# Output stage of a hybrid encoder block: the split activations kept in pieces of 32 tokens instead of 16

## The reference, cut to what matters

```python
z = jnp.einsum('thed,td->the', expert_u[eidx], tb)
act = (gates * jax.nn.gelu(z.astype(jnp.float32))).astype(tb.dtype)
return jnp.einsum('the,thed->td', act, expert_v[eidx])
```

## Time and profile before

| | us |
|---|---|
| median of 3 runs | 4347.16 |
| lowest and highest of them | 4347.15, 4352.74 |
| the profiled execution's own time | 4347.39 |
| its span, first to last instruction | 4345.8 |
| output stage in it, first to last matmul on `x_split_o` | 3342.2 to 4326.1 |

### The profile page before, as it was taken

One profiled execution on the slowest core, in us unless ns is written; L12 is line 12 of the kernel. 1 busy time (PEld: TensorE's weight loads), 2 busy tenths in 40 slices (PEclk: granted clock), 3 DMA queues, 4 the chain that ended last, 5 costly groups with the idle time before them and its releaser, 6 DMA issues.

```text
span 4345.8 us, 65461 instructions
## 1 busy us (share of the span) xinstructions
PE 4269.3 (98%) x24970; PEld 3904.0 (90%) x24970; DVE 3410.7 (78%) x4173; ACT 1286.6 (30%) x1230; POOL 917.9 (21%) x804
## 2 busy tenths in 40 slices
PE   8999999999999999999999999999999999999998
PEld 5778887989989888887889999999999999999998
DVE  5776766788888844555897999987776989999996
ACT  4222222221222232222223444432333323333333
POOL 0111111000100020011111333344441222222223
PEclk9999999999999999999999999999999999999999
DMA  6888887799888986989844888999997989999995
GB/s 221 302 290 303 288 309 247 252 286 292 282 291 286 320 301 216 306 283 343 282 151 146 325 326 336 354 385 370 370 363 277 353 334 371 362 383 378 376 353 192
DMA packets 395168, 1326.18 MB, mean 305 GB/s; under 512 B 29472, under 2 KB 202528, under 8 KB 279360
## 3 DMA queue, kind: packets, MB, share of 16 engines
q1 hardware_dynamic: 298352, 892.67, 59.3%
q0 software_dynamic: 62224, 391.99, 22.8%
q10 hardware_dynamic: 34496, 40.37, 2.6%
HBM read 1130.49 MB, written 328.53 MB: 336 GB/s over the span
## 4 chain that ended last, share of the span: by engine, by line
PE 81%; DVE 9%; issue 3%; DMA 3%; SPq 1%; POOL 1%; ACT 0%; DVEq 0%; POOLq 0%; ACTq 0%
PE bank L833 26%; PE bank L834 26%; PE bank L835 25%; DVE w_lo L1567 2%; DMA u_rows<-u_turned_c 2%; DVE u_row L2103 1%; DVE hot_j L2113 1%; PE bank L933 1%; PE bank L940 1%; DVE u_turned_c L1574 1%; DVE hot_i L2109 1%; SPq L443 1%; PE bank L1069 1%; PE bank L909 1%; POOL cand L731 0%
## 5 line engine op out<-in xcount | busy, mean ns | idle before, releaser
L833 PE MATMUL bank<-x_hi,w_hi 128*128 128x352 f32 (+2 forms) x5760 | 1942.7, 337 | 15.3 <-DVE w_lo L1567 6.9
L834 PE MATMUL bank<-x_lo,w_hi 128*128 128x352 f32 (+2 forms) x5760 | 1931.0, 335 | 0.0
L835 PE MATMUL bank<-x_hi,w_lo 128*128 128x352 f32 (+2 forms) x5760 | 1929.0, 335 | 0.0
L1154 ACT ACTIVATE w_hi<-w_raw 128x2048 fp32r<-128x2048 f32 x432 | 827.1, 1915 | 1987.9 <-PE bank L835 1887.7
L1567 DVE TENSOR_TENSOR w_lo<-w_raw,w_hi 128x2048 fp32r<-128x2048 f32 x432 | 995.0, 2303 | 259.1 <-ACT w_hi L1154 256.9
L833 PEld LDWEIGHTS bank<-x_hi,w_hi 128*128 128x128 f32 x5760 | 1085.5, 188 | 119.5 <-issue 28.9
L834 PEld LDWEIGHTS bank<-x_lo,w_hi 128*128 128x128 f32 x5760 | 1084.8, 188 | 85.0 <-issue 2.6
L835 PEld LDWEIGHTS bank<-x_hi,w_lo 128*128 128x128 f32 x5760 | 1085.5, 188 | 82.6
L834 PE MATMUL bank<-x_split_o,w_hi 128*128 128x352 f32 x2048 | 657.1, 321 | 0.0
L833 PE MATMUL bank<-x_split_o,w_hi 128*128 128x352 f32 x2048 | 655.5, 320 | 0.8 <-DVE z_group L1992 0.8
L835 PE MATMUL bank<-x_split_o,w_lo 128*128 128x352 f32 x2048 | 654.5, 320 | 0.0
(11 more groups left out here) (309 smaller groups left out, 2849.1 us busy)
## 6 DMA issues: line engine op xcount, KB each, us to landing
v_rows<-v_blocks SPq DMA_DIRECT2D x128, 1024.0 KB, 10.3
w_raw<-u_blocks SPq DMA_DIRECT2D x128, 1024.0 KB, 6.9
w_raw<-v_blocks SPq DMA_DIRECT2D x128, 1024.0 KB, 7.3
w_raw<-w_proj SPq DMA_DIRECT2D x112, 1024.0 KB, 7.3
u_raw_a<-u_blocks SPq DMA_DIRECT2D x99, 1024.0 KB, 8.3
u_rows<-u_turned_a SPq DMA_DIRECT2D x396, 256.0 KB, 5.6
g_scratch<-g_chunk SPq DMA_DIRECT2D x11, 2048.0 KB, 13.2
z_scratch<-z_stage POOLq DMA_DIRECT2D x112, 176.0 KB, 5.3
```

The source lines that it names most:

```text
L833: pe.matmul(dst, whi, xhi, start=start, stop=False)
L834: pe.matmul(dst, whi, xlo, start=False, stop=False)
L835: return pe.matmul(dst, wlo, xhi, start=False, stop=stop)
L1154: act.activation(WH[s][:, :], RAW[s][:, :], ACT.Copy).then_inc(w_hi, 1)
```

## The change

A tile of 352 tokens is now 11 pieces of 32 tokens (128 bytes), 2240 bytes apart. The 16 tiles of a group (8 K-tiles, `hi` and `lo`) lie side by side in each 2240 bytes: tile `t` at `128*t`, with 192 bytes left over. The two groups take 24832 bytes each. The whole begins 32 bytes later (byte 4256; the weights' first byte is 128 above a multiple of 256, this one 160), and `v_row1`, `v_row2` lie 992 bytes lower. The matmuls, their number, widths and order are the same, and so are the weights and their places; on all five engines the order of instructions is what it was, with the shape `11x32` where `11x2x16` stood. One wait has another value: all eight `act_hi` of group 0 now wait until row 11 of `x_hi` (counted from 0) has been read, since every tile reaches over all of the 24640 bytes.

```diff
-PIECE = 16
-ROWS = 12
-TILES = 3
+PIECE = 32
+ROWS = NT // PIECE
+PITCH = 2 * GJ * PIECE + 48
+SPAN = (ROWS * PITCH + 63) // 64 * 64
...
-    (XSO, VG1, VG2), e13 = lay(xh_at, [("x_split_o", [P, (2 * KT + TILES - 1) // TILES, 2, ROWS, TILES, PIECE], F32R),
-                                       ("v_row1", [P, D], F32), ("v_row2", [P, D], F32)])
+    xo_at = xh_at + (raw_at - xh_at + 32) % 256
+    (XSO, VG1, VG2), e13 = lay(xo_at, [("x_split_o", [P, 2, SPAN], F32R), ("v_row1", [P, D], F32),
+                                       ("v_row2", [P, D], F32)])
...
-    def x_o(kk, lo):
-        t = 2 * kk + lo
-        return XSO[:, t // TILES, :, 0:NT // (2 * PIECE), t % TILES, :].rearrange("p i j e -> p j i e")
+    def x_o(par, jj, lo):
+        t = 2 * jj + lo
+        return XSO[:, par, 0:ROWS * PITCH].rearrange("p (j n) -> p j n", n=PITCH)[:, :, t * PIECE:t * PIECE + PIECE]
 
     def in_pieces(a):
-        return a.rearrange("p (j i e) -> p j i e", i=2, e=PIECE)
-
-    def old_tile(kk):
-        return (8 * ROWS * TILES * PIECE * ((2 * kk + 1) // TILES + 1) - 1) // (4 * L)
+        return a.rearrange("p (j e) -> p j e", e=PIECE)
+
+    x_o_old = (xo_at - xh_at + 4 * ROWS * PITCH - 1) // (4 * L)
...
             for jj in range(GJ):
-                act_hi(0, jj, jj + 1, x_free, 4 * (KT - 1) + old_tile(jj) + 1)
+                act_hi(0, jj, jj + 1, x_free, 4 * (KT - 1) + x_o_old + 1)
```

More of the change, by code:

```diff
@@ L1090, in out_block @@
                         m = mm3(o_bank[u][k][:, 0:NT], WH[u][:, wcol], WL[u][:, wcol],
-                                x_o(GJ * par + jj, 0), x_o(GJ * par + jj, 1), jj == 0, jj == GJ - 1)
+                                x_o(par, jj, 0), x_o(par, jj, 1), jj == 0, jj == GJ - 1)
                 m.then_inc(w_used, 1)
@@ L1472, in act_hi @@
                 act.wait_ge(sem_, free)
-                act.activation(x_o(GJ * par + jj, 0), in_pieces(ZG[par][:, jj, :]), ACT.Copy).then_inc(x_hi, 1)
+                act.activation(x_o(par, jj, 0), in_pieces(ZG[par][:, jj, :]), ACT.Copy).then_inc(x_hi, 1)
             for jj in range(GJ):
-                act_hi(0, jj, jj + 1, x_free, 4 * (KT - 1) + old_tile(jj) + 1)
+                act_hi(0, jj, jj + 1, x_free, 4 * (KT - 1) + x_o_old + 1)
             gelu_kept(NB_E - 1)
@@ L2137, in product_lo @@
                 dve.wait_ge(x_hi, x0 + jj + 1)
-                dve.tensor_tensor(x_o(GJ * par + jj, 1), in_pieces(ZG[par][:, jj, :]), x_o(GJ * par + jj, 0).bitcast(F32),
+                dve.tensor_tensor(x_o(par, jj, 1), in_pieces(ZG[par][:, jj, :]), x_o(par, jj, 0).bitcast(F32),
                                   ALU.subtract).then_inc(x_lo, 1)
```

## The result

| | before | after |
|---|---|---|
| median us (runs) | 4347.15 (4) | 4377.14 (4) |
| lowest and highest us | 4346.9, 4352.74 | 4372.8, 4383.1 |
| profiled execution, its span | 4347.39, 4345.8 | 4372.8, 4371.2 |
| first to last matmul on `x_split_o` | 983.9 | 1008.6 |

The ratio is 1.0067 (95% interval 1.0049 to 1.0084): the changed kernel is slower by 0.7%, and 4377.14 us lies above the whole range that was given (to 4362).

What follows compares the result with a forecast made beforehand. PE was taken as the bound. 4347.4 - 1.5 (slow K-tile) + 1.9 (wait) + 1.1 (clock) = 4348.9 us, less 0.2 to the median: 4348.7 us, +0.04%. Own range 4342 to 4355, whole range 4334 to 4362.

Steps and rivals of the forecast that it cites:

- What bounds the kernel: PE, busy 978.6 of 981 us in the output stage; 1 ns on each of 6144 matmuls is 6.1 us.
- Instructions: Number, order and widths stay; ACT's and DVE's splits gain 8 and 3 ns at most, off the bound: nothing.
- (a): Moving reads, 11 jumps for 22: at most 34.5 us less, taken as zero because straight tiles are slower.
- (b): Moving reads against the weight load beside each matmul: taken as zero, bounds +11 us and -17 us.
- straight rate: Z stage's 159.7 ns per matmul with tiles in one run; +1.8 ns, +11 us, taken as upper bound.
- (c): Odd groups' slow K-tile 2, blamed on pieces either side of byte 32768: loss goes, 1.5 us less.
- The wait at the changeover: Group 0's splits on ACT wait for row 11, so PE restarts 1.9 us late, near 3344.1.
- The clock after that pause: PE idle 2.7 us at the changeover, then one fall to half clock: 1.1 us more, bounds 0 and 2.4.
- B: Rival, output stage: longer pieces collide like a straight run, 11 us more, 4360 us; far end 4374; chance 0.26.
- D: Rival: layout is nothing to PE, only wait and clock remain, 4350.2 us; chance 0.12.

Runs made afterwards that it cites:

- e6: Changed kernel with pieces 2176 bytes apart (even groups) and 2304 (odd) instead of 2240: 160.0 / 164.5 ns per matmul, total 4378.95 us.
- e8: Old pieces of 16 tokens in the changed kernel's address order modulo 256 (even groups), second half 128 on (odd): 163.1 / 163.3 ns, 4381.92 us.
- e7: Changed kernel, split weights and all after w_raw 64 bytes on, pieces 128 (even) / 192 (odd) from weights modulo 256: 162.2 / 166.7 ns, 4392.07 us.
- e9: Changed kernel with a weight load of 32 columns instead of 128: 161.1 ns in both kinds of group, 4380.77 us.
- f1: Changed kernel, pieces 192 (even) / 0 (odd) bytes from weights modulo 256, weight load of 32 columns: 160.0 / 163.0 ns, 4372.83 us.
- f4: Kernel before, each piece of 16 beginning 64 bytes back (even groups) or 32 back (odd) modulo 256: 163.3 / 159.5 ns, 4376.8 us.
- g1: Kernel before with a stretch's tiles 256 bytes apart instead of 64, all at place 0: 155.6 ns, median 4338.99 against 4355.16 us, ratio 0.9977.
- e10: Kernel before with a weight load of 32 columns instead of 128: 158.6 / 158.4 ns (even / odd groups), 4349.06 us.
- e2: Changed kernel with pieces 96 (even groups) / 128 (odd) bytes from the weights modulo 256 instead of 32: 162.2 ns in both, 4384.69 us.
- e3: Changed kernel with pieces 160 (even groups) / 192 (odd) bytes from the weights modulo 256 instead of 32: 163.8 / 166.6 ns, 4399.34 us.
- e5: Changed kernel with pieces 2048 bytes apart (even groups) and 2112 (odd) instead of 2240: 164.5 / 165.6 ns, 4397.61 us.
- e1: Changed kernel with pieces 0 (even groups) / 64 (odd) bytes from the weights modulo 256 instead of 32: 164.4 / 162.3 ns, 4383.36 us.
- e4: Changed kernel with pieces 224 (even groups) / 32 (odd, unchanged) bytes from the weights modulo 256: 162.2 ns in both, 4377.75 us.
- e12: Kernel before, with the step after each pair of pieces 0 (even groups) or 64 forward (odd) instead of 64 back: 165.8 / 166.9 ns, 4404.39 us.
- f2: Kernel before's order, hi at 0 and lo at 64 (even groups), both at 0 (odd), halves 25344 bytes apart: 157.8 / 155.6 ns late, 4347.55 us.
- f3: Kernel before's order, hi 64 and lo 0 (even groups), hi 128 and lo 64 (odd), halves 25344 bytes apart: 158.8 / 157.9 ns, 4366.95 us.
- g2: Kernel before with all tiles at place 64 from the weights modulo 256: 155.6 ns, median 4351.59 against 4355.16 us, ratio 0.9998.

## Why the prediction was wrong, point by point

**What bounds the kernel: right.** 1 ns on each matmul was put at 6.1 us. Measured: 4.0 ns in the trace and 24.6 us in the stage.

**Instructions: right.** The splits kept their cost and order; DVE is busy 883.2 us of the stage (882.0 before), ACT 302.2 (303.6):
```profile
3345.00:4351.00 1006.00, 1003.73 (x6186) 1003.41 (x6185) 883.20 (x807) 302.17 (x266) 268.19 (x177) 1.00 0.88 337
```

**(a) Jumps cost nothing: right.** e6's even groups have eleven pieces and the rate of a straight tile, and e8 has the old 22 pieces and about the new rate.

**(b) The pattern against the weight load: this step failed.** It took zero, because a step of 64 back was kept, and bounded the loss by the straight rate, +1.8 ns or 11 us. The loss was 4.0 ns, 24.6 us. The two reads do act on each other (e7 with e9 and f1), so the kind of effect was right. What was wrong is to take the slope for a sufficient reason: e8 and f4's odd groups have it too, and stand at 163.1 and 159.5. The text saw the difference ("a piece sweeps 128 bytes once instead of 64 bytes twice") and set it aside in favour of the row nearest. And the straight tile was no upper bound: it is one order among others, and most kernels of the table are slower than it.

**(c) The slow K-tile: right in its size, wrong in its cause.** It was 11 to 13 ns slower than its neighbours (582 ticks of 1/1.2 ns against 566 to 569), as the 12 taken. But byte 32768 did not make it. In g1 the same tile lies over that byte, also with pieces on both sides of it in turn, and its K-tile takes 560 ticks like all others. And e10 moves the slow one to other K-tiles with all moving addresses kept: there it is even K-tile 2, none of whose bytes lies near that address. (In the kernel before, only the first four of the tile's eleven pairs lie on either side of the byte, not all as the prediction reads.) The 1.5 us were no gain of their own; every K-tile became as slow as that one, 0.486 us.

**The wait at the changeover: right.** Forecast 1.9 us, measured 2.1 (last Z matmul to first output matmul 1.1 us before, 3.2 after). ACT and DVE of after, as the earlier trace rows, then PE, as the earlier trace rows:
```profile
3338.27 3.21 ACT L1474 ACTIVATE x_split_o<-z_group 128x352 fp32r<-128x352 f32 x8 [3.46 <-PE bank L836]
3341.39 1.90 ACT L1155 ACTIVATE w_hi<-w_raw 128x2048 fp32r<-128x2048 f32 x1
```
```profile
3338.80 3.57 DVE L2139 TENSOR_TENSOR x_split_o<-z_group,x_split_o 128x352 fp32r<-128x352 f32 x8 [2.05 <-ACT x_split_o L1474]
3342.29 0.52 DVE L1993 TENSOR_TENSOR z_group<-bank,rstd_b 128x352 f32<-128x352 f32 x1
```
```profile
3337.85 0.32 PE L836 MATMUL bank<-x_hi,w_lo 128*128 128x352 f32 x1
...
3339.77 0.32 PE L836 MATMUL bank<-x_hi,w_lo 128*128 128x352 f32 x1
3342.96 0.43 PE L834 MATMUL bank<-x_split_o,w_hi 128*128 128x352 f32 x1 [2.87 <-DVE z_group L1993]
```
The eight splits are one piece, begun 0.42 us after the third matmul of row 11 (3337.85), as worked out; PE stands still for 2.87 us (forecast 2.7). The 0.2 us more are DVE's: its eight `product_lo` take 3.57 us in a row where ACT's eight take 3.21, so they end last by their own pace and not by ACT's eighth, which the prediction followed. The weight split and the evacuation behind it are hidden, as was said.

**The clock after that pause: 0 by luck, and the fall was priced too low.** Forecast +1.1 us, measured 0. In after, the window behind the restart holds 21 matmuls at the upper level, and only the later stretch, which the kernel before has too, is at half:
```profile
3345.00:3348.00 3.00, 3.00 (x21) 1.00 1.10 382
...
3549.70:3556.40 6.70, 6.70 (x29) 0.50 0.94 371
```
Other executions did fall at this very pause. The restart of e2, and the window around it:
```profile
3350.74 0.66 PE L836 MATMUL bank<-x_split_o,w_hi 128*128 128x352 f32 x1 [2.84 <-DVE z_group L1995]
```
```profile
3350.00:3356.70 6.70, 5.96 (x20) 0.50 0.93 335
```
e2, e3 and e9 fell to half after 2.8 us of idle time and e5 after 2.4, while after, e1, e4, e6, e7 and f1 kept the upper level after 2.8 to 2.9. The last Z block before the pause is the same in all of them, and so is the work behind it, but for the layout and the shorter load of e9 and f1. So neither the idle time nor the work around it tells whether the clock falls; what does stays open. Where it fell, the first output block took 1.2 us (e9) to 2.8 us (e2) longer than the second, 0.1 of it also without a fall. The forecast's 1.1 lies at the lower end, and e2 is beyond its bound of 2.4; its fall is most of the 4.1 us by which its stage is longer than that of after at the same interval. It was read off a window of 13 matmuls, of which ten are of the kind `bank<-hot_j,hot_i` with 128 columns: no measure for matmuls of 352.

**The rivals.** B named the right sign and, at its far end (162 ns, +25 us, 4374 us), the size: that end was read off the slow K-tile, whose rate every K-tile now has. Its reason, longer pieces that collide like a straight run, falls with e6 (straight order, 160.0) and e8 (short pieces, 163.1). The range cut B at the straight rate; with that far end inside it would have held the profiled time, and 4377 us still not. D, that the layout is nothing to PE, is refuted. The Trainium skill says in "SBUF — State Buffer", section "Who interferes with whom", that PE's two read ports are independent and that PE never waits. Here, with instructions and transfers alike, the interval reached from 155.6 (g1) to 166.9 ns (e12) with only the addresses changed, and the measurement decides. The 149.2 ns that D took from the Trainium skill, "TensorE: Matmul & The Clock Gate", section "Back-to-back issue gap", is given there for an isolated matmul and not for a stream with weight loads, so it does not say that this stage has no surplus; no kernel here came below 155.6.

## What to carry to other kernels

Where PE is the bound and streams its moving tile beside a weight load, the addresses of the moving tile modulo 256 bytes can be worth several per cent of the interval: 7% between the best and the worst here, for fp32r and 352 columns. Best was to have all moving tiles at one place. Take any new layout as unknown until its rate is measured, and measure it in several stretches and more than one execution, since one layout can have two rates. Count matmuls in a window rather than compare totals, which spread by more than most of these effects. And when a layout's rate is to be bounded, the other pattern at hand is a sample, not an upper bound; a cause inferred from the address of one slow tile wants an experiment of its own.

## What the hardware showed beyond that

**A rhythm in whole ticks.** The intervals are not a smooth average. In the changed kernel the three matmuls of a K-tile start 157.5, 165.8 and 163.3 ns apart, 584 ticks of 1/1.2 ns in all, in every group and every K-tile on average. g1 has 560 ticks, the straight order 576, the kernel before 566 to 572 with a slow one of 582. It looks as if the stream settles into a repeating state.

**One layout, two rates.** That state does not follow from the addresses alone. f2's odd groups went from 160.0 to 155.6 ns with the pause of PE in group 3 between, the code and all addresses being the same. Even groups changed as well: 162.2 in group 0 and 163.8 from group 2 on in e3, 167.8 and 165.6 in e12, 157.8 and 158.9 in f3. What was traced in two executions came out alike in both, though: 162.2 at place 32 (after, e4) and at 128 (e2, e7), 166.6 and 166.7 at 192 (e3, e7), 155.6 with all tiles at one place (g1, g2). The kernel before was traced once, but the times of all its runs, up to 4360.15 us, and those of the changed kernel, from 4372.8, do not overlap, so the loss stands. f2's change of 4.4 ns is as large as that loss, though: a kernel that was traced once (e5, e6, e8, e12, f1, f3, f4) shows a rate that its layout can have, and not that it has no other.

**One code, two rates.** The last two fifths of the Z stage, whose code and addresses are the same in all kernels but e7, hold 1252 matmuls in 200 us in some executions and 1235 in others. Two windows of e3, and one of after for comparison:
```profile
2900.00:3100.00 200.00, 200.00 (x1235) 1.00 0.95 372
3100.00:3300.00 200.00, 200.00 (x1235) 1.00 0.91 357
```
```profile
2900.00:3100.00 200.00, 200.00 (x1252) 1.00 0.97 380
```
160.0 against 162.2 ns (576 and 584 ticks) from about block 74 of 128 on, 54 x 48 = 2600 matmuls, is 5.8 us, nearly half of the 13 us by which runs of the kernel before differ. e2, e3, e9, e12, f3 and f4 ran at the slower rate, and so did e7. e5 and e8 changed the other way near the same block, from 162.2 to 160.0. In e3 the change comes with a short stop of PE, 324 ns between two starts at 2926.7. What decides between the rates stays open. As the output stage too has more than one rate for one layout (f2), this may be part of the spread of g1's and g2's runs, of which one each was traced.
